# Two transformer blocks on one core: another order of products, norm sums and residuals at the stage boundaries

## What is computed

```
# first block
z = rms_norm(h, g_mix_pre) @ w_in            # then conv, attention, pooling branches
h = h + rms_norm(mix, g_mix_post)            # post-norm "p1"
ff = square(relu(rms_norm(h, g_mlp_pre) @ w_up)) @ w_down
h = h + rms_norm(ff, g_mlp_post)             # post-norm "p2"
e = (p @ w_ple_proj) * sigmoid(rms_norm(h, g_ple_pre) @ w_ple_gate)
h = h + rms_norm(e, g_ple_post)              # post-norm "p3"
# second block
z = rmsnorm(h, ln_mix_g) @ w_in_2            # attention and gated linear attention
x = h + merged @ w_out_2
x = x + (silu(conv(a)) * u) @ w_ffn_out_2    # a, u = rmsnorm(x, ln_ffn_g) @ w_ffn_in_2
```

## Time and profile before

| | |
|---|---|
| median of 3 runs | 1494.48 us (1494.46 to 1496.58) |
| profiled execution, its own time | 1495.4 us |
| its span, first to last instruction | 1493.6 us |
| PE busy | 1460.6 us, 98% of the span, 6978 matmul records |
| DVE, ACT, POOL busy | 54%, 38%, 17% |
| chain that ended last | 86% on PE, 6% DVE, 2% ACT, 2% POOL |
| mean granted TensorE clock | 0.989 of 2.4 GHz |

### The profile page before, as it was taken

One profiled execution on the slowest core, in us unless ns is written; L12 is line 12 of the kernel. 1 busy time (PEld: TensorE's weight loads), 2 busy tenths in 40 slices (PEclk: granted clock), 3 DMA queues, 4 the chain that ended last, 5 costly groups with the idle time before them and its releaser, 6 DMA issues.

```text
span 1493.6 us, 17745 instructions
## 1 busy us (share of the span) xinstructions
PE 1460.6 (98%) x6978; PEld 1192.0 (80%) x6978; DVE 809.7 (54%) x1167; ACT 560.6 (38%) x829; POOL 254.2 (17%) x170
## 2 busy tenths in 40 slices
PE   9999989999999999899999999999999999999998
PEld 7866768888888887677789887788887888888887
DVE  5688465433333357574678734634535665534564
ACT  5345434523323125433355545322224443323310
POOL 4234344301101013340033203100003000000000
PEclk9999999999999999998999999999999999999999
DMA  6221222432333332211211111333332233232331
GB/s 228 88 68 57 71 71 71 121 105 85 101 97 99 99 96 74 85 57 57 71 43 58 51 35 43 113 94 93 96 102 82 74 113 110 87 111 85 99 100 69
DMA packets 36131, 129.18 MB, mean 86 GB/s; under 512 B 4024, under 2 KB 4280, under 8 KB 36048
## 3 DMA queue, kind: packets, MB, share of 16 engines
q1 hardware_dynamic: 35760, 127.78, 27.7%
q10 hardware_dynamic: 288, 0.26, 0.1%
HBM read 125.91 MB, written 2.10 MB: 86 GB/s over the span
## 4 chain that ended last, share of the span: by engine, by line
PE 86%; DVE 6%; ACT 2%; POOL 2%; issue 2%; DMA 0%; ACTq 0%; POOLq 0%; DVEq 0%
PE P L1073 25%; PE P L1075 25%; PE P L1074 25%; PE P L1332 1%; PE P L1114 1%; DVE P L1886 1%; POOL AC L2363 1%; PE P L1115 1%; PE P L1116 1%; PE P L1218 1%; DVE WL L1732 1%; POOL H L2372 1%; PE P L1294 1%; PE P L1169 1%; POOL DD L2363 1%
## 5 line engine op out<-in xcount | busy, mean ns | idle before, releaser
L1073 PE MATMUL P<-AH,WH 128*128 128x512 f32 x1104 | 445.5, 404 | 8.9 <-issue 4.4
L1074 PE MATMUL P<-AL,WH 128*128 128x512 f32 x1104 | 434.3, 393 | 0.0
L1075 PE MATMUL P<-AH,WL 128*128 128x512 f32 x1104 | 434.3, 393 | 0.0
L1412 ACT ACTIVATE WH<-WR 128x1024 fp32r<-128x1024 f32 x232 | 243.8, 1051 | 337.0 <-PE P L1075 321.6
L1732 DVE TENSOR_TENSOR WL<-WR,WH 128x1024 fp32r<-128x1024 f32 x215 | 279.0, 1298 | 158.8 <-ACT WH L1412 158.3
L1073 PEld LDWEIGHTS P<-AH,WH 128*128 128x128 f32 x1104 | 210.1, 190 | 62.8 <-issue 14.2
L1075 PEld LDWEIGHTS P<-AH,WL 128*128 128x128 f32 x1104 | 209.8, 190 | 45.0
L1074 PEld LDWEIGHTS P<-AL,WH 128*128 128x128 f32 x1104 | 210.1, 190 | 42.4 <-issue 0.7
L1075 PE MATMUL P<-FH,WL 128*128 128x512 f32 x432 | 168.1, 389 | 0.0
L1073 PE MATMUL P<-FH,WH 128*128 128x512 f32 x432 | 168.1, 389 | 0.0
L1074 PE MATMUL P<-FL,WH 128*128 128x512 f32 x432 | 168.1, 389 | 0.0
(11 more groups left out here) (320 smaller groups left out, 1873.8 us busy)
## 6 DMA issues: line engine op xcount, KB each, us to landing
WR<-in_ws SPq DMA_DIRECT2D x232, 512.0 KB, 3.6
out<-Y SPq DMA_DIRECT2D x8, 256.0 KB, 2.0
H<-in_xT SPq DMA_DIRECT2D x3, 512.0 KB, 8.2
C<-in_const SPq DMA_DIRECT2D x1, 946.5 KB, 11.1
H<-in_xT SPq DMA_DIRECT2D x2, 256.0 KB, 4.1
PR<-in_pT SPq DMA_DIRECT2D x1, 512.0 KB, 4.6
WR<-in_ws SPq DMA_DIRECT2D x1, 384.0 KB, 4.4
WR<-in_ws ACTq DMA_DIRECT2D x1, 128.0 KB, 3.8
```

The source lines that it names most:

```text
L1073: e.matmul(P, wh, xh, start=start, stop=False)
L1074: e.matmul(P, wh, xl, start=False, stop=False)
L1075: ins = e.matmul(P, wl, xh, start=False, stop=stop)
L1412: e.activation(m.WH[:, c % NW, :], m.WR[:, c % NRAW, :], ACT.Copy).then_inc(*at.up("w_hi", "w_hi", c))
```

## The change

- **Split products in heads.** New steps `mm_hi` (the two products with `AH`) and `mm_lo` (the one with `AL`). A head issues `mm_hi` of block j for all tiles, then `mm_lo` of block j - 1 for all tiles; the last `mm_lo` stands at the end. `sums` now stands after `mm_hi` of block 7, before `mm_lo` of blocks 6 and 7. The buffer of a chunk is given back by `mm_lo`.
- **Five tiles** in every head, so in head 3 too.
- **Direct squares.** In p1 and p3, `direct` is 3: squares 5, 6 and 7 get tiles of their own and are summed on PE. The `warm` of three matmuls ahead of `sums` is gone from p1 and p3.
- **Residual 1** is added on DVE, as 0, 2, 4 and 6 are.
- **Head 5.** `x_hi`, `x_lo` and `square` of blocks 0 to 5 are made during the last product of the stage before, and 6 and 7 in the first two rounds of the head.
- **Newton start.** One tiny instruction (the shift) is folded into the next.

```diff
@@ def head
-        else:
+        elif s != "5":
             make(0)
             make(1)
             rest(0)
-        rest(1)
-        make(2)
-        got = [self.ring() for _ in range(3)] + [self.bank(b) for b in (6, 7)[:len(specs) - 4]]
+        if s != "5":
+            rest(1)
+            make(2)
+        got = [self.ring() for _ in range(3)] + [self.bank(b) for b in (6, 7)]
+        behind = []
         for j in range(8):
+            ids = []
+            for m, t in enumerate(got):
+                ids.append(self.weight(specs[m][j]))
+                self.say("mm_hi", t, ids[m], (x, j), j == 0)
             if j == 7:
                 self.sums(s, 0)
-            for m, t in enumerate(got):
-                self.block(t, specs[m][j], (x, j), j == 0, j == 7)
+            behind.append((ids, j))
+            for ids, i in behind[:1 if j else 0]:
+                for m, t in enumerate(got):
+                    self.say("mm_lo", t, ids[m], (x, i), False)
+                behind = behind[1:]
+            if s == "5":
+                if j < 2:
+                    make(j + 6)
+                    rest(j + 6)
+                continue
             if j < 5:
                 make(j + 3)
             if j < 6:
                 rest(j + 2)
+        for m, t in enumerate(got):
+            self.say("mm_lo", t, behind[0][0][m], (x, 7), True)
         b = self.spread(s)
-        out = got + [self.tile(specs[len(got)], [(x, j) for j in range(8)])]
+        out = got + [self.tile(q, [(x, j) for j in range(8)]) for q in specs[5:]]
         self.say("rbc", s, b)
@@ def post
-        if fill is None:
-            self.say("warm", self.bank(6), 3)
         self.sums(n, direct)
@@ def mixer1, and the same for p3 in mlp1
-                    self.say("square", "p1", m, 1)
+                    self.say("square", "p1", m, 3)
-        return self.post("p1", 1)
+        return self.post("p1", 3)
@@ def mixer2, in the loop over the tiles of w_out_2
+            if 0 < m < 7:
+                self.say("x_hi", "5", m - 1)
+                self.say("x_lo", "5", m - 1)
+                self.say("square", "5", m - 1, 0)
@@ class Memory
+    def square(self, n, i, direct):
+        SQ, AC = self.sq(n)
+        if direct == 3 and i >= 5:
+            return SQ[:, 1, :] if i == 7 else self.post(n)[1][:, i - 5, :]
+        return AC if i == 0 else SQ[:, i % 2, :]
@@ tensor_program
+    def mm_hi(t, i, x, start):
+        c, o = i // CH, (i % CH) * 128
+        P, xh = m.bank[t.bank][:], m.x(*x)[0]
+        part = int(o >= FIRST)
+        w.wait_ge(*(at("w_hi", c) if c else at("w_hi0", part)))
+        w.wait_ge(*at("x_hi", *x))
+        if start:
+            free(t)
+        e.matmul(P, m.WH[:, c % NW, o:o + 128], xh, start=start, stop=False)
+        w.wait_ge(*(at("w_lo", c) if c else at("w_lo0", part)))
+        e.matmul(P, m.WL[:, c % NW, o:o + 128], xh, start=False, stop=False)
+    def mm_lo(t, i, x, stop):
+        c, wh, wl, ends = weights(i)
+        w.wait_ge(*at("x_lo", *x))
+        ins = e.matmul(m.bank[t.bank][:], wh, m.x(*x)[1], start=False, stop=stop)
+        if stop:
+            ins.then_inc(*at.up("full", "full", t.id))
+            if ends:
+                at.also(("full", t.id), "w_used", c)
+        elif ends:
+            ins.then_inc(*at.up("w_used", "w_used", c))
@@ sums, on PE
-        if direct:
-            w.wait_ge(*at("square", n, 7))
+        for i in range(8 - direct, 8):
+            w.wait_ge(*at("square", n, i))
+            S = m.square(n, i, direct)
             for q in range(4):
-                ins = e.matmul(P[:, q:q + 1], SQ[:, 1, 128 * q:128 * q + 128], one, start=False, stop=True,
+                ins = e.matmul(P[:, q:q + 1], S[:, 128 * q:128 * q + 128], one, start=False, stop=i == 7,
                                skip_group_check=True)
@@ rsqrt, on DVE
-        e.tensor_scalar(u.bitcast(I32), v.bitcast(I32), 1, None, ALU.logical_shift_right).then_inc(
-            *at.up("newton", "root1", name))
-        w.wait_ge(*at("root1", name))
-        e.tensor_scalar(y.bitcast(I32), u.bitcast(I32), -1.0, float(0x5F3759DF), ALU.mult, ALU.add).then_inc(
+        e.tensor_scalar(y.bitcast(I32), v.bitcast(I32), -0.5, float(0x5F3759DF), ALU.mult, ALU.add).then_inc(
@@ residual, on DVE
-        if i % 2 == 0:
+        if i % 2 == 0 or i == 1:
```

More of the change, by code:

```diff
@@ L537, in mlp1 @@
                 self.say("ple_gated", m - 1)
-                self.say("square", "p3", m - 1, 1)
+                self.say("square", "p3", m - 1, 3)
         for m in (6, 7):
             self.say("ple_gated", m)
-            self.say("square", "p3", m, 1)
-        return self.post("p3", 1)
+            self.say("square", "p3", m, 3)
+        return self.post("p3", 3)
     def mixer2(self, ready):
@@ L1157, in sums @@
     def sums(n, t, direct):
-        SQ, AC = m.sq(n)
+        AC = m.sq(n)[1]
         if first[0]:
@@ L1394, in gn_spread @@
         spread_to(m.bank[t.bank], m.roots("gn", 16)[1][:, 4 * hh:4 * hh + 4]).then_inc(*at.up("full", "full", t.id))
-    run = {"mm": mm, "mm_tokens": mm_tokens, "mm_values": mm_values, "mm_narrow": mm_narrow, "warm_first": warm_first, "warm": warm, "sums": sums, "spread": spread,
+    run = {"mm": mm, "mm_hi": mm_hi, "mm_lo": mm_lo, "mm_tokens": mm_tokens, "mm_values": mm_values, "mm_narrow": mm_narrow, "warm_first": warm_first, "warm": warm, "sums": sums, "spread": spread,
            "scores1": scores1, "turn1": turn1, "values1": values1, "ln_mean": ln_mean, "ln_center": ln_center,
@@ L1429, in square @@
     def square(n, i, direct):
-        SQ, AC = m.sq(n)
         w.wait_ge(*at("summand", n, i))
-        if i >= 3:
+        if direct == 3 and i >= 5:
+            w.wait_ge(*at("summed", n, 3))
+        elif i >= 3:
             w.wait_ge(*at("summed", n, i - 2))
-        e.activation(AC if i == 0 else SQ[:, i % 2, :], m.summed(n, i), ACT.Square).then_inc(
+        e.activation(m.square(n, i, direct), m.summed(n, i), ACT.Square).then_inc(
             *at.up("square", "square", n, i))
```

## The result

The changed kernel takes 1502.95 us, the median of six runs (1500.80 to 1506.14), against 1495.21 for the kernel before beside it (1493.78 to 1498.43): a ratio of **1.0048, 95% interval 1.0033 to 1.0064**, or 7.7 us slower. The forecast was +7.0 and 1501.5. The profiled execution is the longest of the six, 1506.14 with a span of 1504.3, so 10.7 us lie between the two traces, three more than between the medians.

What follows compares the result with a forecast made beforehand. PE bounds the kernel, busy 1460.6 of 1493.6 us. Stages at full clock (3.6 - 0.3 - 3.3 - 0.2 + 1.2 = +1.0) plus clock falls (+6.0) give 1494.48 + 7.0 = 1501.5, range 1494 to 1508.

Steps and rivals of the forecast that it cites:

- `sums` to `spread` with the last `w_lo` ahead of Newton: In each head `spread` starts 6.3 us after `sums` (6.1 in heads 1 and 5), PE waiting 3.0 or 2.8.
- Head 1: Start to `spread` of head 1: earlier start, new 1.3 us wait for `w_lo`, `spread` at 39.45 against 35.85, +3.6.
- Post p1 and head 2: Three direct squares and a start on `x_hi` gain 3.3 us, given back by head 2's `spread`: 241.9 against 242.21, -0.3.
- The removed `warm` cost nothing, since POOL was later than it: In p1, dropping the `warm` ahead of `sums` adds no time, because POOL's additions ended later.
- Head 3: Start 0.85 us earlier, and the fifth tile covers PE's 3.29 us wait for POOL at `sums`: -3.3.
- Post p3 and head 4: Reckoned like p1: start 3.3 us earlier, low clock at head 4's start kept, `spread` 674.4 against 674.6, -0.2.
- Head 5: The 1.65 us wait at head 5's start goes; `spread` comes at 1158.4 against 1157.15, +1.2.
- The clock: Behind the five new waits at `spread`, 0.7 of them cost a clock fall of 1.7 us: +6.0, ends 0 and 8.5.
- The clock falls at every new wait: Rival: falls behind all five waits at `spread` and behind head 3's first matmul: +10.0, 1504.5; chance 0.18.
- the clock stays up: Rival: no clock fall behind the new waits, gains of the starts balance them: +0.5, 1495; chance 0.17.
- The last `w_lo` does not hold Newton: Rival: the buffer is free earlier, so the five waits at `spread` go: -13.6, 1481, or 1483 where DVE is late; chance 0.09.
- The helpers fall behind: Rival: `w_hi` waits longer for its buffer ahead of `x_hi` on ACT, delaying `sums` in heads 1 to 4: 1507; chance 0.08.

Runs made afterwards that it cites:

- the hold: The changed kernel with each head's last `w_lo` queued behind the Newton steps instead of ahead of them: 1487.18 us, ratio 0.9952 to the kernel before.

## Why the prediction was right, and where it was wrong

The forecast was the case that came: 1502.95 inside 1494 to 1508, slower by over 0.2%, 1.5 us above the 1501.5. By its steps:

- **`sums` to `spread` with the last `w_lo` ahead of Newton: right**, and the hold shows that it is the cause. Forecast 6.3 us in head 2, measured 6.37; forecast waits 3.0 and 2.8, measured 2.92, 2.89, 2.92 and 2.69, 2.66; sum 14.6 against 14.1. The step that did it was counting which low product gives back the buffer, and seeing on which side of `sums` it stands.
- **Head 1: right within 0.6** (+3.6, measured +4.2). The wait for `w_lo` of block 8 was 0.76, not 1.3. That `w_lo` was ready at 12.51 instead of 12.1, for the ACT queue had waited 0.4 us longer for a load of `H`, and PE came to it at 11.8 instead of 10.8, after two short stops.
- **Post p1 and head 2: the sum failed, -0.3 against +2.9.** The chain from the first residual to PE's first matmul was right: forecast 2.3 us, measured 216.25 to 218.53. What failed is "Four groups of columns on PE at 0.9" and "The removed `warm` cost nothing, since POOL was later than it". The groups took 5.3 us instead of 3.6, since the clock fell in their middle, and `spread` came a us behind Newton because the four remaining warm matmuls took 3.53. "POOL was later than it" was true and beside the point: behind PE's wait without them the clock fell, and their removal from the kernel before costs 4.5 us. In the changed kernel putting them back did not help. The step that failed is thus the clock in the post, which the sum had at 1.00 without a term for it, as the one trace of the kernel before showed it; other executions of the same post have 0.87. Why it falls in that row was not isolated.
- **Head 3: right** (-3.3, measured -3.4).
- **Post p3 and head 4: failed, -0.2 against +4.0.** "As p1" was the error. p3's squares come out of a chain of gating on DVE and ACT that begins at head 3's `spread`. A fifth tile ahead of `spread` leaves one tile fewer in which this chain runs, and its last link was 3.1 instead of 0.8 us behind the last tile. The prediction counted the fifth tile's gain at head 3's `sums` and did not ask what it does to the next stage. Back at four tiles, the wait went from 3.0 to 0.7 us, and the gain of head 3 with it. The 1.6 us of low clock that the sum kept for the start of head 4 did not come either: the clock was 1.00 over the four us behind its first matmul, and low in the post instead (0.66).
- **Head 5: right** (its `spread` +2.7 against +2.85). The stretch before it gained 4.3 us where 1.65 were counted; 1.4 of the rest lies in mixer 2, at a slightly higher clock.
- **The clock: right in kind.** 0.7 of five falls at 1.7 us, 6.0, were forecast; the changed kernel's execution shows two of five, worth 1.6 and 2.9 us, and another kernel with the same waits four of five.
- So the size was met by luck as well, errors that cancel: the two posts with the heads behind them came out 7.4 us dearer, the clock behind `spread` 1.5 cheaper and the stretch before head 5 2.6 cheaper, and the median lies 3 us nearer to the kernel before than the profiled execution does.

**The rivals.** "The clock falls at every new wait" and "the clock stays up" were both wrong as rules: falls are two and four in five. The Trainium skill, "TensorE: Matmul & The Clock Gate", Part 1, has it that the throttled state is the default and that activity lifts it. The trace without the warm matmuls agrees, with a clock of 0.66 over the ten us that hold an idle stretch of 3.25. Read with the profile's busy time, that rule would have kept the clock up in post p1 of the changed kernel, 9.57 of 10 us; the trace shows 0.66, so there the measurement decides. "The last `w_lo` does not hold Newton" was wrong for this kernel, and right as a price: its 14.6 us for the waits are what the hold gave back (14 to 16). Its time of 1481 was still 6 us too low, by the posts. "The helpers fall behind" did not come: PE waited for POOL 0.8 us in heads 2, 3 and 4, and not in heads 1 and 5. Of the signs that the prediction named, one failed: the first matmul of heads 2 and 4 was to come 3 us earlier behind the last tile, and came 0.4 earlier and 1.5 later.

## What to carry to other kernels

When products are moved behind a step that something waits for, follow the buffers they give back: a helper's next job may stand ahead of the very instruction that the moved step was to feed, and an in-order queue turns it into a wait. Before removing filler from a wait, ask not only whether it is on the path, but what runs right behind the wait and at which clock. And before an idle stretch is filled with work from a later stage, look for what that work was covering there: here the fifth tile carried most of the gap with it.

## What the runs showed of the hardware

- TensorE can be busy by its records and lose its clock. In post p1 of the changed kernel, in a row of 32 one-column matmuls (5.3 us, PE busy for 9.57 of 10 us), the granted clock fell to 0.66 over ten us, that is, to the 1.2 GHz level for most of them, and a group of eight went from 1.02 to 1.84 us. With warm matmuls in front it fell too, a group later. It also fell in two of four executions that have this post as in the kernel before, with 16 such matmuls.
- Six matmuls that only multiply constants, in the shadow of a wait at each of two posts (3.3 and 4.0 us without them), are worth 0.30% of the kernel before (0.17 to 0.43). The traces show 2.5 and 2.0 us at the two posts, but the same posts vary by up to 0.9 and 1.9 us with no edit to them.
- The same stretch of 1525 matmuls with the same idle time took from 240.8 to 250.2 us in the kernels of this study, at a granted clock of 0.98 to 0.94.
